# A hybrid decoder layer on one core: the order of work around the first pair of the feed-forward part

## The chip, the cores and the metric

One core of one Trainium2 chip runs the whole layer in one launch. The metric is the device time of a run in microseconds (us); several runs are timed and their median is given. One more execution is recorded by the profiler, and its time stands beside its span (from the first to the last instruction).

## What is computed

The input x has 512 tokens of 1024 channels. A layer norms it, projects it, runs four token mixers beside each other, merges them by gates, projects back and adds. Then comes the feed-forward part (FFN), which is what the change touches:

```python
def swiglu_ffn(h, w_gate, w_up, w_down):
    return (jax.nn.silu(h @ w_gate) * (h @ w_up)) @ w_down

x = x + merged @ w_out
h = rms_norm(x, ffn_norm[l])          # this is h2 below
x = x + swiglu_ffn(h, w_ffn_gate[l], w_ffn_up[l], w_ffn_down[l])
```

All is float32. D_FF is 2816.

## The kernel before

**Three products for one.** A float32 matrix is split into a high part in a reduced format that TensorE multiplies fast (made by ScalarE, ACT, with a copy) and a low part, the rest (made by VectorE, DVE, with a subtraction of the high part). One product is then three matmuls on TensorE (PE): high by high, high by low, low by high. So every operand of PE needs an ACT instruction, then a DVE instruction.

**h2.** The normed x is scaled by DVE (`scaled`, L1976), one tile of 128 tokens after another, t = 0 to 3. `turn_h2(t)` (L2669) is eight transposes on PE into two banks of PSUM, four for each; ACT makes the high part `f_hi` of each bank (`h2_high`, L1230), DVE the low part `f_lo` (`h2_low`, L1944). Tiles 0 and 1 are turned during the output projection, tiles 2 and 3 during the plain part below, at the place in the loop where the `if` at its end says so.

**The first pair, plain.** The FFN weights come in chunks of 256 columns, a gate chunk and an up chunk for each pair. The first pair is multiplied the plain way: `plain_part(up, half)` (L2716) does both column tiles (j = 0, 1) of one chunk for one half of the tokens, 8 steps k of 3 matmuls for each j, in the order gate/first half, up/first half, gate/second half, up/second half. Then ACT takes the gate tiles with Silu (`gated`, L1338, adds to `gate_taken`) and DVE multiplies them with the up tiles (`hidden`, L2111, adds to `up_taken`).

**The other pairs, Winograd.** `wino_chunk(c)` (L2747) does each further chunk as seven products of half-size blocks, 12 matmuls each. In order: 1 A11·B11, 2 S3·T3, 3 S2·T2, 4 A12·B21, 5 S1·T1, 6 A22·T4, 7 S4·B22. The T are sums of blocks of h2: `block_sums` (DVE, L2045 to L2055) makes the four, `block_high` (ACT, L1348) their high parts, `t_low` (DVE, L2059) their low parts, in the order T3, T2, T1, T4. The S are sums of blocks of the chunk's weights: `weight_sums` (DVE, L2070 to L2077; its step 0 is the first two, step 1 the other two). High parts of weights are made by ACT in four steps (`wino_split`, L1317 to L1326), low parts by DVE in four steps (`weight_lows`: step 0 L2084, step 1 L2089, steps 2 and 3 L2095). `split_ahead` does the steps of the next chunk while PE works on this one.

**Sums through PSUM.** Between the products, results are copied from bank to bank: after product 1 ACT seeds c11 (L1414); after product 2 ACT copies `seventh` (L1419); after product 3 DVE adds c21 (L2226, semaphore `c21_seeded`), for which PE waits ahead of product 5; after product 5 ACT copies c12 (L1428, `c12_seeded`), for which PE waits ahead of product 7; after product 6 DVE adds c22 (L2244).

**What sets the order.** Every engine has one list of instructions in the order of the code, and does them strictly in that order; semaphores hold an engine until another has come far enough. Nothing is scheduled by a planner. In ACT's list, in the first Winograd chunk (m = 0) alone, the high parts of the first hidden tiles stand ahead of the copy of c12:

```python
                split_ahead(c + 1, 1, 2, 3)
                if m == 0:
                    for j in range(CT):
                        hidden_high(0, j, j + 1)
                act.wait_ge(S["product_done"], 7 * m + 5)
                nact.activation(f0[:, T2ND], first[:, T1ST], ACT.Copy).then_inc(S["c12_seeded"], 1)
```

`hidden_high(0, j, j + 1)` (L1344) waits until `up_taken` has reached j + 1, that is for the (j + 1)th `hidden` of DVE.

Of the kernel before, what the change touches and what calls it, by code (L numbers as in the profile page):

```python
# [42 lines left out]
def hybrid_layer(nc, x, mix_norm, w_in, attn_q_norm, attn_k_norm, pool_w, pool_scale, gmlp_norm,  # L43
# [5 lines left out]
    KT = D // P  # L49
# [127 lines left out]
    WINO = [c for c in range(NC) if chunks[c][0] == "ffn"]  # L177
# [60 lines left out]
    with ExitStack() as ctx:  # L238
# [626 lines left out]
        def _(act):  # L865
# [462 lines left out]
            def split_ahead(c, *steps):  # L1328
                if c < NC and chunks[c][0] == "ffn":
                    for step in steps:  # L1330
                        wino_split(c, step)
                elif c < NC and 0 in steps:
                    split(c)
# [12 lines left out]
            def block_high(i):  # L1346
                act.wait_ge(S["t_made"], 4)
                nact.activation(t_hi[:, i], t_sum[:, i], ACT.Copy).then_inc(S["t_hi_ready"], 1)  # L1348
# [44 lines left out]
                split_ahead(part_at[1], 0, 1, 2, 3)  # L1393

            T1, T2, T3, T4 = range(4)
            act.wait_ge(filled, fill_at[PLAIN[0]] + 1)
            gated(0, 0, bank[2])
            block_high(T3)
            block_high(T2)
            act.wait_ge(filled, fill_at[PLAIN[0]] + CT)  # L1400
            gated(0, 1, bank[3])
            split_ahead(WINO[0], 0, 1)
            split_ahead(WINO[0], 2)
            block_high(T1)
            split_ahead(WINO[0], 3)
            block_high(T4)

            for c in WINO:
                m = wino_index[c]
                pair, up = pair_of(c)  # L1410
# [71 lines left out]
        def _(dve):  # L1482
# [574 lines left out]
            def t_low(i):  # L2057
                dve.wait_ge(S["t_hi_ready"], (T3, T2, T1, T4).index(i) + 1)
                vec.tensor_tensor(t_lo[:, i], t_sum[:, i], t_hi[:, i].bitcast(F32), ALU.subtract)\  # L2059
                    .then_inc(S["t_lo_ready"], 1)  # L2060
# [37 lines left out]
            def split_ahead(c, *steps):  # L2098
                if c < NC and chunks[c][0] == "ffn":
                    for step in steps:  # L2100
                        weight_lows(c, step)
                elif c < NC and 0 in steps:
                    split(c)
# [89 lines left out]

            block_sums()
            t_low(T3)
            dve.wait_ge(lo_ready, PLAIN[1] + 1)
            sums_ahead(WINO[0])
            split_ahead(WINO[0], 0)
            split_ahead(WINO[0], 2)
            t_low(T2)  # L2200
            split_ahead(WINO[0], 1)
            t_low(T1)
            split_ahead(WINO[0], 3)
            t_low(T4)

            for c in WINO:
# [19 lines left out]
                vec.tensor_tensor(f1[:, T1ST], first[:, T1ST], seventh[:, up, :], ALU.add).then_inc(S["c21_seeded"], 1)  # L2226
                if m == 0:
                    weight_sums(c + 1, (1,))
                    for j in range(CT):
                        dve.wait_ge(filled, fill_at[PLAIN[1]] + j + 1)  # L2230
                        hidden(0, j, bank[(fill_at[PLAIN[1]] + j) % 2])
                    split_ahead(c + 1, 0, 1)
                else:
                    split_ahead(c + 1, 0, 1, 2, 3)
                if c == F11 - 1:
# [7 lines left out]
                dve.wait_ge(S["c12_seeded"], m + 1)  # L2243
                vec.tensor_tensor(f1[:, T2ND], first[:, T1ST], seventh[:, up, :], ALU.add).then_inc(S["c22_ready"], 1)  # L2244
                if m == 0:
                    split_ahead(c + 1, 2, 3)
                if c == F11 - 2:

                    dve.wait_ge(S["up_taken"], CT * 2 * QT // CT)
# [72 lines left out]
        def _(pe):  # L2322
# [393 lines left out]
            def plain_part(up, half):  # L2716

                c = PLAIN[up]
                at = w_at(c)
                c_hi, c_lo = (p1_hi[:, :], p1_lo[:, :]) if up else (w_hi[:, at + HIGH_OFF:at + HIGH_OFF + CHUNK],  # L2720
                                                                    w_lo[:, at:at + CHUNK])
                cols = slice(half * SEQ // 2, (half + 1) * SEQ // 2)
                pe.wait_ge(hi_ready, c + 1)
                if up:
                    pe.wait_ge(S["out_lo"], len(OUT_SPLIT) + 1)
                else:
                    pe.wait_ge(lo_ready, c + 1)
                pe.wait_ge(S["h2_lo_ready"], TT * (half + 1) - 1)
                pe.wait_ge(S["x1_taken"], (8, OUT_ADDS)[up])
                for j in range(CT):  # L2730
                    b = bank[(fill_at[c] + j) % 2] if up else bank[2 + j]
                    for k in range(KT):
                        if j == 0 and k == KT // 2:
                            pe.wait_ge(S["h2_lo_ready"], TT * (half + 1))
                        w = slice(k * CW + j * P, k * CW + (j + 1) * P)
                        begin, end = k == 0 and half == 0, k == KT - 1
                        mm(b[:, cols], c_hi[:, w], f_hi[:, k, cols], start=begin, stop=False, skip_group_check=True)  # L2737
                        mm(b[:, cols], c_hi[:, w], f_lo[:, k, cols], start=False, stop=False, skip_group_check=True)  # L2738
                        last = mm(b[:, cols], c_lo[:, w], f_hi[:, k, cols], start=False, stop=end, skip_group_check=True)  # L2739
                        if up and (half, j) == (0, 0) and k in (0, KT // 2):  # L2740
                            turn_h2(2 + k // (KT // 2))
                    if half == 1:
                        last.then_inc(filled, 1)

# [119 lines left out]
```

## Time and profile before

| | |
|---|---|
| median of 3 runs | 759.77 us (759.62 to 760.0) |
| the profiled execution, its own time | 759.43 us |
| its span | 757.5 us |
| PE busy | 750.8 us (99%) |
| DVE busy | 591.0 us (78%) |
| ACT busy | 404.0 us (53%) |
| POOL busy | 105.4 us (14%) |
| granted clock of PE in the span | 1.00 |

A time of the profile is counted from the start of the span. The device time is the span and about 1.9 us around it. In the timeline a row is one instruction, or several alike (x2), with its start, its length, its line and its tiles; what stands in brackets is how long the engine had been idle and what released it. Matmuls overlap: a matmul of 256 columns is shown as 0.28 us long, while the next starts 0.11 us after it. The distance between the starts of two neighbours is called their spacing below. On DVE and ACT too, an instruction may start a little before the one ahead of it is shown as ended.

### The profile page before, as it was taken

The numbers are of one execution on the slowest core, as the hardware profiler recorded it, in microseconds if no ns is written. First come the engines' busy times: TensorE is split into PE (matmuls) and PEld (weight loads), VectorE is DVE, ScalarE is ACT, GpSimd is POOL, SyncE is SP. The second block draws the span as 40 slices with busy tenths as digits, with TensorE's granted clock in tenths as the row PEclk, the third lists the DMA queues.
The fourth block names the chain that finished last, engine by engine and source line by source line (L and its number), as shares of the span: only waits on it lengthen the run. The fifth ranks groups of instructions, "written<-read, shape, count | busy, mean of one in ns | idle before, by whom it ended". The sixth has DMA issues, their size and how long they took to land.

```text
span 757.5 us, 11636 instructions
## 1 busy us (share of the span) xinstructions
PE 750.8 (99%) x4590; PEld 665.7 (88%) x4590; DVE 591.0 (78%) x816; ACT 404.0 (53%) x603; POOL 105.4 (14%) x130
## 2 busy tenths in 40 slices
PE   8999999999999999999999999999999999999998
PEld 8988888988888888888888899999888999999886
DVE  5636989878788966425988889889989888888991
ACT  6645546456663654545349555565544556666430
POOL 7100040457203221221231000000000000000000
PEclk9999999999999999999999999999999999999999
DMA  8362213221133113317226624336063333338102
GB/s 280 100 188 73 92 58 112 69 100 55 56 112 111 56 60 109 112 55 274 88 85 174 186 112 137 109 105 236 0 250 112 112 113 112 112 113 315 73 29 84
DMA packets 67879, 89.56 MB, mean 118 GB/s; under 512 B 3109, under 2 KB 52593, under 8 KB 67697
## 3 DMA queue, kind: packets, MB, share of 16 engines
q1 hardware_dynamic: 66224, 85.60, 33.6%
q0 software_dynamic: 1456, 3.09, 2.0%
q8 instruction: 37, 0.61, 0.3%
q10 hardware_dynamic: 144, 0.13, 0.1%
q14 instruction: 18, 0.14, 0.1%
HBM read 81.99 MB, written 4.19 MB: 114 GB/s over the span
## 4 chain that ended last, share of the span: by engine, by line
PE 96%; DVE 1%; ACT 1%; issue 1%; POOL 1%; DVEq 0%; POOLq 0%
PE bank L2327 14%; PE bank L2329 14%; PE bank L2328 14%; PE bank L2765 8%; PE bank L2766 8%; PE bank L2767 8%; PE bank L2827 5%; PE bank L2831 5%; PE bank L2829 5%; PE bank L2708 2%; PE bank L2707 2%; PE bank L2706 2%; PE bank L2737 1%; PE bank L2738 1%; PE bank L2739 1%
## 5 line engine op out<-in xcount | busy, mean ns | idle before, releaser
L2327 PE MATMUL bank<-h_hi,w_hi 128*128 128x512 f32 (+1 forms) x352 | 134.7, 383 | 0.2 <-DVE w_lo L1569 0.2
L2329 PE MATMUL bank<-h_hi,w_lo 128*128 128x512 f32 (+1 forms) x352 | 133.7, 380 | 0.0
L2328 PE MATMUL bank<-h_lo,w_hi 128*128 128x512 f32 (+1 forms) x352 | 133.6, 379 | 0.0
L1497 DVE TENSOR_TENSOR w_lo<-raw,w_hi 128x2048 fp32r<-128x2048 f32 x30 | 71.0, 2371 | 39.7 <-ACT w_hi L881 31.8
L2765 PE MATMUL bank<-t_hi,w_hi 128*128 128x256 f32 x320 | 88.4, 276 | 1.1 <-DVE bank L2226 1.1
L2766 PE MATMUL bank<-t_lo,w_hi 128*128 128x256 f32 x320 | 88.3, 276 | 0.0
L2767 PE MATMUL bank<-t_hi,w_lo 128*128 128x256 f32 x320 | 88.3, 276 | 0.0
L2327 PEld LDWEIGHTS bank<-h_hi,w_hi 128*128 128x128 f32 x352 | 66.2, 188 | 12.6 <-ACT w_hi L944 0.4
L2329 PEld LDWEIGHTS bank<-h_hi,w_lo 128*128 128x128 f32 x352 | 66.2, 188 | 12.6
L2328 PEld LDWEIGHTS bank<-h_lo,w_hi 128*128 128x128 f32 x352 | 66.2, 188 | 12.1
L2765 PE MATMUL bank<-f_hi,w_hi 128*128 128x256 f32 x240 | 66.4, 277 | 0.3 <-ACT bank L1428 0.3
L2766 PE MATMUL bank<-f_lo,w_hi 128*128 128x256 f32 x240 | 66.3, 276 | 0.0
L2767 PE MATMUL bank<-f_hi,w_lo 128*128 128x256 f32 x240 | 66.3, 276 | 0.0
L2765 PEld LDWEIGHTS bank<-t_hi,w_hi 128*128 128x128 f32 x320 | 60.1, 188 | 1.3 <-issue 1.3
L2767 PEld LDWEIGHTS bank<-t_hi,w_lo 128*128 128x128 f32 x320 | 60.1, 188 | 0.0
L2766 PEld LDWEIGHTS bank<-t_lo,w_hi 128*128 128x128 f32 x320 | 60.1, 188 | 0.0
L849 POOL TENSOR_TENSOR merged<-merged,two 128x512 f32<-128x512 f32 x24 | 37.3, 1558 | 161.9 <-DVE two L1875 161.9
L881 ACT ACTIVATE w_hi<-raw 128x2048 fp32r<-128x2048 f32 x28 | 53.8, 1925 | 0.2 <-DMA raw<-in_w_in_dram 0.2
L1071 ACT ACTIVATE two<-bank 128x512 f32<-128x512 f32 x24 | 14.4, 599 | 65.0 <-PE bank L2329 58.3
L2095 DVE TENSOR_TENSOR w_lo<-w_sum,w_hi 128x1024 fp32r<-128x1024 f32 x40 | 47.1, 1217 | 0.0
L2827 PE MATMUL bank<-w_hi,a_hi 128*128 128x512 f32 x120 | 46.8, 390 | 0.0
L2829 PE MATMUL bank<-w_lo,a_hi 128*128 128x512 f32 x120 | 46.7, 389 | 0.0
(357 smaller groups left out, 1862.4 us busy)
## 6 DMA issues: line engine op xcount, KB each, us to landing
raw<-in_w_in_dram SPq DMA_DIRECT2D x26, 1024.0 KB, 4.9
raw<-in_w_ffn_up_dram SPq DMA_DIRECT2D x11, 1024.0 KB, 5.1
raw<-in_w_ffn_gate_dram SPq DMA_DIRECT2D x10, 1024.0 KB, 5.1
raw<-in_w_ffn_down_dram SPq DMA_DIRECT2D x7, 1024.0 KB, 5.0
raw<-in_w_branch_dram SPq DMA_DIRECT2D x4, 1024.0 KB, 4.7
b<-in_w_ffn_down_dram SPq DMA_DIRECT2D x4, 1024.0 KB, 6.8
x_sb<-in_x_dram SPq DMA_DIRECT2D x6, 512.0 KB, 4.6
o<-in_w_out_dram SPq DMA_DIRECT2D x3, 1024.0 KB, 9.9
```

The costliest lines, as they stand in the source:

```text
L881: nact.activation(w_hi[:, at:at + n], raw[:, c % 2, 0:n], ACT.Copy).then_inc(hi_ready, 1)
L1497: vec.tensor_tensor(w_lo[:, at], raw[:, c % 2, 0:n], w_hi[:, high].bitcast(F32), ALU.subtract)\
L2095: vec.tensor_tensor(quad(w_lo, c, s, 2), quad(w_sum, c, s, 2), quad(w_hi, c, s, 2).bitcast(F32), ALU.subtract).then_inc(S["quad_lo_ready"], 1)
L2327: mm(dst, l_hi, r_hi, start=start, stop=False)
L2328: mm(dst, l_hi, r_lo, start=False, stop=False)
L2329: return mm(dst, l_lo, r_hi, start=False, stop=stop)
L2765: mm(dst, l_hi, r_hi, start=begin and k == 0, stop=False, skip_group_check=True)
L2766: mm(dst, l_hi, r_lo, start=False, stop=False, skip_group_check=True)
L2767: ins = mm(dst, l_lo, r_hi, start=False, stop=k == KT // 2 - 1, skip_group_check=True)
L2827: mm(bank[banks[t]][:, :], l_hi[:, k, rows], w_hi[:, w], start=anew and k == 0, stop=False, skip_group_check=True)
L2829: mm(bank[banks[t]][:, :], l_hi[:, k, rows], w_lo[:, w], start=False, stop=False, skip_group_check=True)
L2831: ins = mm(bank[banks[t]][:, :], l_lo[:, k, rows], w_hi[:, w], start=False, stop=k == tiles - 1, skip_group_check=True)
```

## The change

It moves instructions on three engines; none is added or taken out.

- PE: `turn_h2(2)` stood after step k = 0 of the first tile of the up chunk, and now stands after step k = 4 of the last tile (j = 1) of the gate chunk, which is 12 matmuls sooner. `turn_h2(3)` stood after step k = 4 of the up chunk's first tile and now stands after step k = 1: 9 matmuls sooner.
- ACT: the high parts of T3, T2 and T1 stand ahead of both gate tiles; before, T3 and T2 stood between the two, and T1 between the steps of the first Winograd chunk's weights.
- DVE: the low parts of T3, T2 and T1 stand in a row ahead of the sums of the first Winograd chunk's weights. In that chunk, steps 0 and 2 of the next chunk's low parts stand ahead of the two `hidden`; before, they stood behind them.

```diff
--- before.py
+++ after.py
@@ -1393,16 +1393,14 @@
                 split_ahead(part_at[1], 0, 1, 2, 3)
 
             T1, T2, T3, T4 = range(4)
+            block_high(T3)
+            block_high(T2)
+            block_high(T1)
             act.wait_ge(filled, fill_at[PLAIN[0]] + 1)
             gated(0, 0, bank[2])
-            block_high(T3)
-            block_high(T2)
             act.wait_ge(filled, fill_at[PLAIN[0]] + CT)
             gated(0, 1, bank[3])
-            split_ahead(WINO[0], 0, 1)
-            split_ahead(WINO[0], 2)
-            block_high(T1)
-            split_ahead(WINO[0], 3)
+            split_ahead(WINO[0], 0, 1, 2, 3)
             block_high(T4)
 
             for c in WINO:
@@ -2193,14 +2191,11 @@
 
             block_sums()
             t_low(T3)
+            t_low(T2)
+            t_low(T1)
             dve.wait_ge(lo_ready, PLAIN[1] + 1)
             sums_ahead(WINO[0])
-            split_ahead(WINO[0], 0)
-            split_ahead(WINO[0], 2)
-            t_low(T2)
-            split_ahead(WINO[0], 1)
-            t_low(T1)
-            split_ahead(WINO[0], 3)
+            split_ahead(WINO[0], 0, 2, 1, 3)
             t_low(T4)
 
             for c in WINO:
@@ -2226,10 +2221,11 @@
                 vec.tensor_tensor(f1[:, T1ST], first[:, T1ST], seventh[:, up, :], ALU.add).then_inc(S["c21_seeded"], 1)
                 if m == 0:
                     weight_sums(c + 1, (1,))
+                    split_ahead(c + 1, 0, 2)
                     for j in range(CT):
                         dve.wait_ge(filled, fill_at[PLAIN[1]] + j + 1)
                         hidden(0, j, bank[(fill_at[PLAIN[1]] + j) % 2])
-                    split_ahead(c + 1, 0, 1)
+                    split_ahead(c + 1, 1)
                 else:
                     split_ahead(c + 1, 0, 1, 2, 3)
                 if c == F11 - 1:
@@ -2243,7 +2239,7 @@
                 dve.wait_ge(S["c12_seeded"], m + 1)
                 vec.tensor_tensor(f1[:, T2ND], first[:, T1ST], seventh[:, up, :], ALU.add).then_inc(S["c22_ready"], 1)
                 if m == 0:
-                    split_ahead(c + 1, 2, 3)
+                    split_ahead(c + 1, 3)
                 if c == F11 - 2:
 
                     dve.wait_ge(S["up_taken"], CT * 2 * QT // CT)
@@ -2737,8 +2733,10 @@
                         mm(b[:, cols], c_hi[:, w], f_hi[:, k, cols], start=begin, stop=False, skip_group_check=True)
                         mm(b[:, cols], c_hi[:, w], f_lo[:, k, cols], start=False, stop=False, skip_group_check=True)
                         last = mm(b[:, cols], c_lo[:, w], f_hi[:, k, cols], start=False, stop=end, skip_group_check=True)
-                        if up and (half, j) == (0, 0) and k in (0, KT // 2):
-                            turn_h2(2 + k // (KT // 2))
+                        if (up, half, j, k) == (0, 0, 1, KT // 2):
+                            turn_h2(2)
+                        elif (up, half, j, k) == (1, 0, 0, 1):
+                            turn_h2(3)
                     if half == 1:
                         last.then_inc(filled, 1)
 
```

How the lists change, first DVE ahead of the first Winograd chunk. `t_lo` are the low parts of T, `w_sum` the sums of the weights' blocks, `w_lo` low parts of weights. Before:

```order
L2059 TENSOR_TENSOR t_lo<-t_sum,t_hi 128x1024 [waits t_hi_ready]
L2070 TENSOR_TENSOR w_sum<-raw 128x512 [waits filled,raw1,lo_ready]
L2071 TENSOR_TENSOR w_sum<-raw 128x512
L2075 TENSOR_TENSOR w_sum<-w_sum,raw 128x512 [waits sum_made]
L2077 TENSOR_TENSOR w_sum<-raw,w_sum 128x512 [waits sum_made]
L2084 TENSOR_TENSOR w_lo<-raw,w_hi 128x1024 [waits quad_hi_ready]
L2095 TENSOR_TENSOR w_lo<-w_sum,w_hi 128x1024 [waits quad_hi_ready,sum_made]
L2059 TENSOR_TENSOR t_lo<-t_sum,t_hi 128x1024 [waits t_hi_ready]
L2089 TENSOR_TENSOR w_lo<-raw,w_hi 128x512 [waits hi_ready]
L2059 TENSOR_TENSOR t_lo<-t_sum,t_hi 128x1024 [waits t_hi_ready]
L2095 TENSOR_TENSOR w_lo<-w_sum,w_hi 128x1024 [waits quad_hi_ready,sum_made]
L2059 TENSOR_TENSOR t_lo<-t_sum,t_hi 128x1024 [waits t_hi_ready]
```

Now (the file is two to five lines shorter, so its numbers are lower):

```order
L2057 TENSOR_TENSOR t_lo<-t_sum,t_hi 128x1024 [waits t_hi_ready] x3
L2068 TENSOR_TENSOR w_sum<-raw 128x512 [waits filled,raw1,lo_ready]
L2069 TENSOR_TENSOR w_sum<-raw 128x512
L2073 TENSOR_TENSOR w_sum<-w_sum,raw 128x512 [waits sum_made]
L2075 TENSOR_TENSOR w_sum<-raw,w_sum 128x512 [waits sum_made]
L2082 TENSOR_TENSOR w_lo<-raw,w_hi 128x1024 [waits quad_hi_ready]
L2093 TENSOR_TENSOR w_lo<-w_sum,w_hi 128x1024 [waits quad_hi_ready,sum_made]
L2087 TENSOR_TENSOR w_lo<-raw,w_hi 128x512 [waits hi_ready]
L2093 TENSOR_TENSOR w_lo<-w_sum,w_hi 128x1024 [waits quad_hi_ready,sum_made]
L2057 TENSOR_TENSOR t_lo<-t_sum,t_hi 128x1024 [waits t_hi_ready]
```

The second and third `t_lo` went ahead of the four sums; the fourth stayed behind.

DVE in the first Winograd chunk, `a_sum` being the two `hidden` of the plain pair. Before:

```order
L2070 TENSOR_TENSOR w_sum<-raw 128x512 [waits filled,raw0]
L2071 TENSOR_TENSOR w_sum<-raw 128x512
L2226 TENSOR_TENSOR bank<-bank,seventh 128x256 [waits gate_taken,seventh_copied,product_done]
L2075 TENSOR_TENSOR w_sum<-w_sum,raw 128x512 [waits sum_made]
L2077 TENSOR_TENSOR w_sum<-raw,w_sum 128x512 [waits sum_made]
L2111 TENSOR_TENSOR a_sum<-bank,act_158 128x512 [waits gate_taken,filled] x2
L2084 TENSOR_TENSOR w_lo<-raw,w_hi 128x1024 [waits quad_hi_ready]
L2089 TENSOR_TENSOR w_lo<-raw,w_hi 128x512 [waits hi_ready]
L2244 TENSOR_TENSOR bank<-bank,seventh 128x256 [waits c12_seeded,product_done]
L2095 TENSOR_TENSOR w_lo<-w_sum,w_hi 128x1024 [waits quad_hi_ready,sum_made] x2
```

Now:

```order
L2068 TENSOR_TENSOR w_sum<-raw 128x512 [waits filled,raw0]
L2069 TENSOR_TENSOR w_sum<-raw 128x512
L2221 TENSOR_TENSOR bank<-bank,seventh 128x256 [waits gate_taken,seventh_copied,product_done]
L2073 TENSOR_TENSOR w_sum<-w_sum,raw 128x512 [waits sum_made]
L2075 TENSOR_TENSOR w_sum<-raw,w_sum 128x512 [waits sum_made]
L2082 TENSOR_TENSOR w_lo<-raw,w_hi 128x1024 [waits quad_hi_ready]
L2093 TENSOR_TENSOR w_lo<-w_sum,w_hi 128x1024 [waits quad_hi_ready,sum_made]
L2109 TENSOR_TENSOR a_sum<-bank,act_158 128x512 [waits gate_taken,filled] x2
L2087 TENSOR_TENSOR w_lo<-raw,w_hi 128x512 [waits hi_ready]
L2240 TENSOR_TENSOR bank<-bank,seventh 128x256 [waits c12_seeded,product_done]
L2093 TENSOR_TENSOR w_lo<-w_sum,w_hi 128x1024 [waits quad_hi_ready,sum_made]
```

Two `w_lo` of 1024 columns (steps 0 and 2) stand ahead of the two `a_sum`; one of 512 (step 1) and one of 1024 (step 3) stand behind them.

ACT, from the last high parts of h2 to the first copy between banks. `act_158` is a gate tile. Before:

```order
L1230 ACTIVATE f_hi<-bank 128x4x128 [waits h2_turned] x4
L1338 ACTIVATE act_158<-bank 128x512 [waits filled,out_tile]
L1348 ACTIVATE t_hi<-t_sum 128x1024 [waits t_made] x2
L1338 ACTIVATE act_158<-bank 128x512 [waits filled]
L1317 ACTIVATE w_hi<-raw 128x1024 [waits filled,raw1]
L1320 ACTIVATE w_hi<-raw 128x512
L1323 ACTIVATE w_hi<-w_sum 128x1024 [waits sum_made]
L1348 ACTIVATE t_hi<-t_sum 128x1024 [waits t_made]
L1326 ACTIVATE w_hi<-w_sum 128x1024 [waits sum_made]
L1348 ACTIVATE t_hi<-t_sum 128x1024 [waits t_made]
L1414 ACTIVATE bank<-bank 128x256 [waits gate_taken,product_done]
```

Now:

```order
L1230 ACTIVATE f_hi<-bank 128x4x128 [waits h2_turned] x4
L1348 ACTIVATE t_hi<-t_sum 128x1024 [waits t_made,out_tile]
L1348 ACTIVATE t_hi<-t_sum 128x1024 [waits t_made] x2
L1338 ACTIVATE act_158<-bank 128x512 [waits filled] x2
L1317 ACTIVATE w_hi<-raw 128x1024 [waits filled,raw1]
L1320 ACTIVATE w_hi<-raw 128x512
L1323 ACTIVATE w_hi<-w_sum 128x1024 [waits sum_made]
L1326 ACTIVATE w_hi<-w_sum 128x1024 [waits sum_made]
L1348 ACTIVATE t_hi<-t_sum 128x1024 [waits t_made]
L1412 ACTIVATE bank<-bank 128x256 [waits gate_taken,product_done]
```

Three `t_hi` stand ahead of the first gate tile. Behind this piece ACT's list is the same in both.

## Rows read from the trace of the kernel before

**Rows 1.** The page of the profile: its head, and the busy time of each engine

```profile
span 757.5 us, 11636 instructions
...
PE 750.8 (99%) x4590; PEld 665.7 (88%) x4590; DVE 591.0 (78%) x816; ACT 404.0 (53%) x603; POOL 105.4 (14%) x130
```

**Rows 2.** Waits of PE over the span: total us, times, longest

```profile
PE bank L2765 <- DVE bank L2226: 1.1, 1, 1.1
...
PE bank L2765 <- ACT bank L1428: 0.3, 1, 0.3
```

**Rows 3.** Timeline of PE, first Winograd chunk: start us, us, operation, [idle before <-releaser]

```profile
452.67 0.28 PE L2765 MATMUL bank<-f_hi,w_hi 128*128 128x256 f32 x1
...
458.00 0.28 PE L2767 MATMUL bank<-f_hi,w_lo 128*128 128x256 f32 x1
459.37 0.36 PE L2765 MATMUL bank<-t_hi,w_hi 128*128 128x256 f32 x1 [1.10 <-DVE bank L2226]
...
462.07 0.28 PE L2767 MATMUL bank<-t_hi,w_lo 128*128 128x256 f32 x1
462.68 0.39 PE L2765 MATMUL bank<-f_hi,w_hi 128*128 128x256 f32 x1 [0.34 <-ACT bank L1428]
```

**Rows 4.** The chain of waits, two pieces: start us, us, engine, tile, line

```profile
460.80 0.89 ACT w_hi L1326
...
461.96 0.40 ACT a_hi L1344
```

**Rows 5.** Timeline of PE: the two groups of transposes of h2

```profile
434.84 1.03 PE L2678 MATMUL bank<-ident,h 128*128 128x128 f32 x8
...
437.13 1.03 PE L2678 MATMUL bank<-ident,h 128*128 128x128 f32 x8
```

**Rows 6.** Timeline of DVE, from the scaling of h2 to the gatings

```profile
433.64 1.28 DVE L1976 SCALAR_TENSOR_TENSOR h<-x_sb,rstd,ffn_gain 128x1024 f32<-128x1024 f32 x1
...
438.40 1.29 DVE L1944 TENSOR_TENSOR f_lo<-bank,f_hi 128x512 fp32r<-128x512 f32 x2 [1.00 <-ACT f_hi L1230]
...
443.38 1.22 DVE L2055 TENSOR_TENSOR t_sum<-h2T,t_sum 128x1024 f32<-128x1024 f32 x1
446.35 1.23 DVE L2059 TENSOR_TENSOR t_lo<-t_sum,t_hi 128x1024 fp32r<-128x1024 f32 x1 [1.76 <-ACT t_hi L1348]
447.53 0.69 DVE L2070 TENSOR_TENSOR w_sum<-raw 128x512 f32<-128x512 f32 x1
...
450.07 1.22 DVE L2084 TENSOR_TENSOR w_lo<-raw,w_hi 128x1024 fp32r<-128x1024 f32 x1
451.21 1.22 DVE L2095 TENSOR_TENSOR w_lo<-w_sum,w_hi 128x1024 fp32r<-128x1024 f32 x1
...
458.69 0.42 DVE L2226 TENSOR_TENSOR bank<-bank,seventh 128x256 f32<-128x256 f32 x1
...
460.35 1.28 DVE L2111 TENSOR_TENSOR a_sum<-bank,act 128x512 f32<-128x512 f32 x2
```

**Rows 7.** Timeline of ACT in the same stretch

```profile
445.27 2.00 ACT L1348 ACTIVATE t_hi<-t_sum 128x1024 fp32r<-128x1024 f32 x2
...
461.66 0.70 ACT L1344 ACTIVATE a_hi<-a_sum 128x256 fp32r<-128x256 f32 x2
462.27 0.36 ACT L1428 ACTIVATE bank<-bank 128x256 f32<-128x256 f32 x1
```

**Rows 8.** Timeline of DVE two chunks later

```profile
473.28 1.33 DVE L2111 TENSOR_TENSOR a_sum<-bank,act 128x512 f32<-128x512 f32 x2
...
478.00 0.43 DVE L2226 TENSOR_TENSOR bank<-bank,seventh 128x256 f32<-128x256 f32 x1 [0.86 <-PE bank L2767]
```

**Rows 9.** Timeline of ACT two chunks later

```profile
474.01 0.42 ACT L1344 ACTIVATE a_hi<-a_sum 128x256 fp32r<-128x256 f32 x1 [2.44 <-DVE a_sum L2111]
```

**Rows 10.** Stretch of the first Winograd chunk: busy of each engine, PEclk, DMA

```profile
452.67:464.10 11.43, 9.99 (x86) 9.63 (x85) 11.39 (x16) 6.19 (x11) 0.00 (x0) 1.00 0.29 93
```

## The prediction

> **What bounds the kernel now.** I read the busy times first: PE is busy for 750.8 of 757.5 us [rows 1]. There is no other bound to look for: the change can win only what PE stands still, or lose by new waits of PE. The table of PE's waits [rows 2] shows how little that is: in the whole FFN part there are two waits, one for DVE's add of c21 (L2226, 1.1 us) and one for ACT's copy of c12 (L1428, 0.3 us). The timeline of PE puts both into the first Winograd chunk and gives their full price [rows 3]. From 452.67 to 458.00 lie 47 spacings, so one is 5.33 / 47 = 0.113 us and a product of 12 matmuls takes 1.36 us. Product 5 could have started at 458.00 + 0.11 = 458.11 and starts at 459.37: 1.26 us lost. Product 7 could have started at 462.07 + 0.11 = 462.18 and starts at 462.68: 0.50 us lost. Between the two, product 5 and 6 took 0.09 us more than 2 x 1.36, since the first matmul after a stop is slow. Without any wait product 7 would start at 458.11 + 2.72 = 460.83; it starts at 462.68. **So 1.85 us, 0.24% of the time, is all that can be won.** I call 0.2%, 1.5 us, what a measurement of this kernel can tell from no change.
>
> Who makes PE wait? DVE has no idle time from 446.35 on [rows 6]; its add of c21 starts at 458.69, although PE's third product was done long before. The chain of waits goes on through ACT: high parts of weights, high parts of the hidden tiles, then the copy of c12 [rows 4]. On ACT the two high parts `a_hi` stand directly ahead of that copy, at 461.66 and 462.27 [rows 7]. That order I follow below, since the change does not alter it.
>
> **The transposes, sooner.** Turn 2 moves up by 12 spacings, from 434.84 [rows 5] to 433.48; turn 3 by 9, at 0.113 to 0.12 us each by 1.02 to 1.08, I take 1.05: from 437.13 to 436.08. PE does the same instructions, so this costs it nothing unless it now waits. Turn 3 needs the last scaling, which starts at 433.64 and ends at 434.92 [rows 6]; 1.16 us are left. Turn 2 needs the scaling before that one, which is ended when this one runs, by about 433.7 at the latest; the scalings are each some 1.2 us apart from the next, so I take it as done by 432.5. Cost: nothing; if the cover were gone, the wait would be about 0.2 us. What turn 3 starts, the low parts of h2 (438.40) and the sums of its blocks (the last at 443.38), follows it by 1.05: the last sum starts at 442.33 and ends at 443.55.
>
> **ACT, three high parts ahead of the gate tiles.** Before, the first T high part started at 445.27 [rows 7], behind a gate tile, although the sums were complete at 443.38 + 1.22 = 444.60 [rows 6]. Now it starts at 443.6. The gate tiles come later by less than the three high parts (0.95 apart, from 2.00 for two), at 446.5 and then as before; nobody needs them before product 1 is done, at 452.67 + 1.36 = 454.03 [rows 3]. Cost: nothing.
>
> **DVE, three low parts ahead of the sums.** The first low part came 1.08 us after its high part's start (445.27 to 446.35) [rows 6, 7], so now at 444.68. Three of them at 1.14 each (450.07 to 451.21 is one instruction of that size) and the weights' sums start at 448.10, where they started at 447.53: 0.57 later. The low part of A11, which product 1 waits for, starts 2.54 us behind that (447.53 to 450.07), at 450.64, and ends at 451.86; PE wants it at 452.67 [rows 3]. 0.8 us of cover are left. From the first sum to the add of c21 lay 458.69 - 447.53 = 11.16 us without idle time; two low parts (2.28) no longer lie there, so it is 8.88, and DVE comes to the add at 456.98. PE's third product ends at 452.67 + 35 x 0.113 + 0.28 = 456.91, so DVE and PE meet. The add comes 1.71 us sooner than before. Its release reached PE 0.68 us later (458.69 to 459.37): 457.66, ahead of 458.11. **The wait ahead of product 5 goes: 1.26 us, and with the slow restart 1.35 us.** That such a lead is enough is seen two chunks later, where the add waits for PE [rows 8] and PE never for it [rows 2].
>
> **DVE, the next low parts ahead of the gatings.** This is the part that costs. Before, the first `hidden` (`a_sum`, L2111) started 1.66 us behind the add of c21 (458.69 to 460.35) [rows 6]. Now two low parts of 1024 columns stand between, 1.14 each: 1.66 + 2.28 = 3.94, so it starts at 456.98 + 3.94 = 460.92, 0.57 later than before, in spite of all that was won. The second follows at 0.60, at 461.52. Behind it stands ACT: `a_hi` starts 0.73 us after its `a_sum` when it waits for it (473.28 to 474.01) [rows 8, 9], so the second at 462.25. Two `a_hi` and the copy of c12 are 0.61 / 2 = 0.31 apart (461.66 to 462.27) [rows 7]: the copy starts at 462.56, where product 5 would allow it from 459.7 on. PE started product 7 0.41 us after the copy's start (462.27 to 462.68) [rows 3, 7]: **462.97, against 462.68 before.** A wait of 2.14 us stands where 1.85 us stood in two.
>
> **The sum.** The stall ahead of product 5: -1.26. The slow restart behind it: -0.09. The stall ahead of product 7: from 0.50 to 462.97 - 460.83 = 2.14, +1.64. Together +0.29 us. What comes behind product 7 follows PE: DVE's steps 1 and 3 of the next chunk end sooner or by 0.3 later than before, and PE wants the last of them only with product 5 of that chunk, some five microseconds on. The bounds of what I had to infer: the hand-over from `a_sum` to `a_hi` is 0.73 where ACT waits and cannot be under the 0.68 that the instruction lasts; the shift of turn 3 is 1.02 to 1.08; the spacing of DVE's instructions may be a few hundredths off over 14 of them. All together -0.2 to +0.4 around the sum. The profiled execution would go from 759.43 to 759.72 us, with a span of 757.8; its own time was 0.34 below the median, and against the median of 759.77 I forecast **760.1 us, no change that can be measured**.
>
> **The clock.** In this stretch the granted clock is 1.00, the level of 2.4 GHz, through stops of 1.10 and 0.34 us [rows 3, 10]. The new stop is longer than either. The Trainium skill says (TensorE: Matmul & The Clock Gate, section "HAM oscillation — how this bites in real kernels") that idle stretches between bursts of matmuls can send the array back to its lower clock. The trace agrees only so far that stops up to 1.10 us did not; by that rule the sum would be as in rival C, by the rows it is +0.29.
>
> **Rivals.**
> A, faster: the gatings' delay does not reach PE, and both waits go. That would be so if the copy of c12 did not stand behind the two `a_hi`, or DVE passed the four instructions much faster. Then 1.85 us are won: 757.9 us. For it speaks that DVE's low parts have to be made anyway and come off the way to c21; against it speaks ACT's strict order in the list and its chain [rows 4, 7]. Between A and my forecast each tenth that DVE gains ahead of the `hidden` is a tenth for PE. Chance 0.05.
> B, the earlier transposes do nothing for the sums (something else, such as ACT's change of table or the scaling, holds the high parts of h2). Then the T sums end at 444.60 as before, the first low part starts at 445.73, and everything down to product 7 is 1.05 us later: 464.0, that is 1.3 over before, 761.1 us. Against it: both turns keep 1 us of cover to the scalings [rows 5, 6]. Chance 0.04, and it stays just within 0.2%.
> C, slower: the stop of 2.14 us ahead of product 7 lets the clock fall to 1.2 GHz. It decides from the first product done at that level: spacing doubles, so each product costs 1.36 us more. Lower end: one product, 0.29 + 1.36 = +1.65, 761.4 us. Upper end: a chunk of seven, +9.8, 769.6. I take the lower end as its price, since the trace has no stretch at the lower level [rows 10] and the nearest stops cost nothing. Chance 0.03.
>
> **How the numbers follow.** My forecast has 0.88: 760.1 us, by its own bounds 759.9 to 760.5, and as the runs before spread over 0.4 us, 759.6 to 760.8. The range reaches to B: 759.5 to 761.1; A and C stay out. Faster by over 0.2%: A, 0.05. Slower by over 0.2%: C and a little of B with a further slip, 0.04. Within: 0.91.
>
> **What the profile would show.** Right: PE's only wait in the first Winograd chunk is for L1426 (the copy of c12 in the new numbers), of about 2 us, and product 5 starts without one; the sums of weights start at about 448.1, the add of c21 at 457.0, the `a_sum` at 460.9, and ACT shows idle time ahead of `a_hi`, released by `a_sum`. Wrong: a copy of c12 that starts before 462; a wait ahead of product 1 or 5; a granted clock under 1.00 behind the stop.

## The result and the profile after

| | before | changed |
|---|---|---|
| median | 759.81 us (20 runs, 759.44 to 760.67) | 761.56 us (20 runs, 759.75 to 762.22) |
| ratio | | 1.0018 (95% interval 1.0012 to 1.0024) |
| profiled execution, its own time | 759.43 us | 759.75 us |
| its span | 757.5 us | 757.8 us |
| runs with a mean granted clock under 0.999 | 2 of 89, beside the experiments below | 13 of 20 |

The change made the kernel slower by 1.75 us in the medians. The runs of the changed kernel do not lie around one value. Seven have a mean granted clock of 1.000 and a median of 759.92 us; thirteen have 0.998 and a median of 761.84. The profiled execution is one of the seven, and its rows are those that were forecast, to a few hundredths of a microsecond. The page of its profile:

```profile
span 757.8 us, 11636 instructions
...
PE 750.2 (99%) x4590; PEld 665.1 (88%) x4590; DVE 591.2 (78%) x816; ACT 404.4 (53%) x603; POOL 105.9 (14%) x130
```

The span is 0.3 us longer. In the table of PE's waits one row stands in the FFN part, where [rows 2] had two:

```profile
PE bank L2763 <- ACT bank L1426: 2.0, 1, 2.0
```

The timeline of PE in the first Winograd chunk (start us, us, operation), which answers to [rows 3]: product 1 begins, product 5 begins, product 6 begins its last matmul, product 7 begins.

```profile
452.59 0.28 PE L2763 MATMUL bank<-f_hi,w_hi 128*128 128x256 f32 x1
...
458.03 0.28 PE L2763 MATMUL bank<-t_hi,w_hi 128*128 128x256 f32 x1
...
460.64 0.28 PE L2765 MATMUL bank<-t_hi,w_lo 128*128 128x256 f32 x1
462.95 0.38 PE L2763 MATMUL bank<-f_hi,w_hi 128*128 128x256 f32 x1 [2.04 <-ACT bank L1426]
```

Product 5 starts on time, 48 spacings behind product 1. Product 7 could start at 460.64 + 0.11 = 460.75 and starts at 462.95: 2.20 us lost in one piece, where before 1.85 were lost in two.

The timeline of DVE, which answers to [rows 6]:

```profile
437.29 1.29 DVE L1942 TENSOR_TENSOR f_lo<-bank,f_hi 128x512 fp32r<-128x512 f32 x2 [1.26 <-ACT f_hi L1230]
...
442.27 1.22 DVE L2053 TENSOR_TENSOR t_sum<-h2T,t_sum 128x1024 f32<-128x1024 f32 x1
444.68 3.50 DVE L2057 TENSOR_TENSOR t_lo<-t_sum,t_hi 128x1024 fp32r<-128x1024 f32 x3 [1.19 <-ACT t_hi L1348]
448.09 0.68 DVE L2068 TENSOR_TENSOR w_sum<-raw 128x512 f32<-128x512 f32 x1
...
456.98 0.42 DVE L2221 TENSOR_TENSOR bank<-bank,seventh 128x256 f32<-128x256 f32 x1
...
458.63 1.22 DVE L2082 TENSOR_TENSOR w_lo<-raw,w_hi 128x1024 fp32r<-128x1024 f32 x1
459.77 1.22 DVE L2093 TENSOR_TENSOR w_lo<-w_sum,w_hi 128x1024 fp32r<-128x1024 f32 x1
460.90 1.28 DVE L2109 TENSOR_TENSOR a_sum<-bank,act 128x512 f32<-128x512 f32 x2
```

The low parts of h2 and the last sum of its blocks (442.27) are 1.11 sooner, of which 0.08 are this execution's earlier start of the whole stretch; the three low parts of T from 444.68, the sums of the weights at 448.09, the add of c21 at 456.98, then the two low parts of 1024 columns ahead of the gatings, and these (`a_sum`) at 460.90.

The timeline of ACT, which answers to [rows 7]:

```profile
443.58 2.96 ACT L1348 ACTIVATE t_hi<-t_sum 128x1024 fp32r<-128x1024 f32 x3 [5.84 <-DVE t_sum L2053]
...
461.62 0.42 ACT L1344 ACTIVATE a_hi<-a_sum 128x256 fp32r<-128x256 f32 x1 [1.58 <-DVE a_sum L2109]
462.21 0.42 ACT L1344 ACTIVATE a_hi<-a_sum 128x256 fp32r<-128x256 f32 x1 [0.18 <-DVE a_sum L2109]
462.54 0.36 ACT L1426 ACTIVATE bank<-bank 128x256 f32<-128x256 f32 x1
```

Both `a_hi` now wait for their `a_sum` (1.58 and 0.18 us idle), and the copy of c12 behind them starts at 462.54, 0.41 ahead of product 7. It was free to start when product 5 ended, at about 459.7.

### The profile page after: what moved, and what is told of

It reads as the page before. It is cut to its first block, busy times and chain, and to the rows that moved or that the text cites. A ratio compares the mean times of both kernels' runs of the same rounds, so it can differ in the third digit from the quotient of the medians.

```text
span 757.8 us, 11636 instructions
## 1 busy us (share of the span) xinstructions
PE 750.2 (99%) x4590; PEld 665.1 (88%) x4590; DVE 591.2 (78%) x816; ACT 404.4 (53%) x603; POOL 105.9 (14%) x130
## 4 chain that ended last, share of the span: by engine, by line
PE 95%; DVE 2%; issue 1%; ACT 1%; POOL 1%; DMA 1%; DVEq 0%; SPq 0%; POOLq 0%
PE bank L2323 14%; PE bank L2325 14%; PE bank L2324 14%; PE bank L2763 8%; PE bank L2764 8%; PE bank L2765 8%; PE bank L2825 5%; PE bank L2827 5%; PE bank L2829 5%; PE bank L2704 2%; PE bank L2703 2%; PE bank L2702 2%; PE bank L2734 1%; PE bank L2735 1%; PE bank L2733 1%
## 5 line engine op out<-in xcount | busy, mean ns | idle before, releaser
L2763 PEld LDWEIGHTS bank<-f_hi,w_hi 128*128 128x128 f32 x240 | 45.1, 188 | 2.3 <-ACT bank L1426 2.2
```

Of the source, the lines that this page charges most:

```text
L2763: mm(dst, l_hi, r_hi, start=begin and k == 0, stop=False, skip_group_check=True)
```

## The experiments

Theory 1: PE's stop of 2.2 us costs its length, and in a part of the executions it also lets the granted clock fall to 1.2 GHz for a while. Rival: the longer executions come from something else in the change. Each kernel was run beside the kernel before on the same chip. In every one the order of some instructions is altered, or matmuls are added whose result nobody reads; all of them compute the whole layer.

**The changed kernel as it is.** No edit, so that a profile of a longer execution could be caught.

> The changed kernel as it is. Theory 1: PE's one stop of about 2.3 us between product 6 and product 7 lets the granted clock fall in some executions; these take about 1.8 us longer. So the times fall into two groups, near 759.9 us with a mean clock of 1.000 and near 761.8 us with 0.998, and a profile from the second shows a stretch of lower clock right behind 463. Rival: the longer executions have another cause (a transfer, a late release elsewhere), and a profile of one shows lost time somewhere else.

Measured: 12 runs, ratio 1.0019 (1.0005 to 1.0033). Six at 1.000 with a median of 760.03 us, six at 0.998 with 762.36. The profile fell on one of the six, with a span of 760.2. Its stretches of 1 us behind the stop (length, busy us of PE, PEld, DVE, ACT, POOL with counts, PEclk, DMA share, GB/s):

```profile
464.00:465.00 1.00, 1.00 (x11) 1.00 (x11) 1.00 (x2) 0.60 (x1) 0.00 (x0) 1.00 0.15 29
465.00:466.00 1.00, 1.00 (x8) 1.00 (x7) 0.69 (x2) 0.45 (x1) 0.00 (x0) 0.51 0.81 236
466.00:467.00 1.00, 1.00 (x6) 1.00 (x6) 1.00 (x3) 0.15 (x1) 0.00 (x0) 0.50 1.09 389
467.00:468.00 1.00, 1.00 (x7) 1.00 (x6) 0.96 (x2) 0.00 (x0) 0.00 (x0) 0.50 1.02 364
468.00:469.00 1.00, 1.00 (x9) 1.00 (x8) 0.24 (x1) 0.89 (x2) 0.00 (x0) 0.78 0.10 32
469.00:470.00 1.00, 1.00 (x11) 1.00 (x10) 0.00 (x0) 0.69 (x2) 0.00 (x0) 1.00 0.00 0
```

And its timeline of PE:

```profile
461.37 0.28 PE L2765 MATMUL bank<-t_hi,w_lo 128*128 128x256 f32 x1
463.71 0.39 PE L2763 MATMUL bank<-f_hi,w_hi 128*128 128x256 f32 x1 [2.06 <-ACT bank L1426]
...
465.31 0.41 PE L2763 MATMUL bank<-f_hi,w_hi 128*128 128x256 f32 x1
465.52 0.41 PE L2764 MATMUL bank<-f_lo,w_hi 128*128 128x256 f32 x1
...
468.49 0.28 PE L2763 MATMUL bank<-t_hi,w_hi 128*128 128x256 f32 x1
468.60 0.28 PE L2764 MATMUL bank<-t_lo,w_hi 128*128 128x256 f32 x1
```

The stop lies from 461.5 to 463.71. PE goes on at full pace, eleven matmuls in the microsecond from 464. At about 465.0 the granted clock falls to 0.50, the spacing goes from 0.113 to 465.52 - 465.31 = 0.21, six to eight matmuls in a microsecond, and at 468.4 it is over. Between 465.10 and 468.49 lie 16 spacings, 3.39 us instead of 1.81: 1.6 us lost. The other 0.8 us by which this span is longer were there before the stop, which lies 0.76 us later than in the first profile (463.71 against 462.95); from run to run the part ahead of the FFN varies by that much. Three more profiles below (the changed kernel again, and the kernels moved by 12 and by 24 matmuls) fell on executions with the lower clock. All four show the same: full pace behind the stop for 0.3 to 1.3 us, then 15 or 16 slow spacings, 1.5 to 1.6 us lost.

The table also shows a burst of transfers in just this stretch. Such a burst is neither enough for the fall nor needed for it. The profile of the changed kernel at full clock has the burst too, without a fall:

```profile
465.50:466.00 0.50, 0.50 (x7) 0.50 (x6) 0.50 (x2) 0.00 (x0) 0.00 (x0) 1.00 1.09 389
```

And in the kernel moved by 24 matmuls the clock is down before the burst begins:

```profile
466.00:466.50 0.50, 0.50 (x5) 0.50 (x4) 0.50 (x2) 0.36 (x1) 0.00 (x0) 0.50 0.00 0
```

The forecast of the stretch holds, the rival falls; what remains to be shown is that the idle time is the cause.

**The stop filled with work.** 16 matmuls between product 6 and the wait.

```diff
                 product(f1[:, T1ST], A22, T4, False)
+                if m == 0:
+                    for _ in range(16):
+                        mm(bank[4][:, T2ND], w_hi[:, w_at(c) + hi_pad(c):w_at(c) + hi_pad(c) + P], t_hi[:, T4, 0, :],
+                           start=True, stop=True, skip_group_check=True)
                 pe.wait_ge(S["c12_seeded"], m + 1)
```

> The changed kernel with 16 more matmuls of 256 columns (1.8 us of work) on PE between product 6 and the wait for c12, into a half of a bank that nobody reads. The wait ends when it did. Theory 1 (the idle of PE is what lets the clock fall): one group of times near 759.9 us, clock 1.000 in every run, though 16 matmuls are added. Rival (the longer group comes from something else in the change): two groups as in the changed kernel, 759.9 and 761.8 us.

Measured: 12 runs, median 760.02 us (759.52 to 760.57), all at 0.999 or 1.000, ratio 1.0000 (0.9992 to 1.0008). Its timeline of PE:

```profile
460.36 0.28 PE L2765 MATMUL bank<-t_hi,w_lo 128*128 128x256 f32 x1
460.47 1.98 PE L2798 MATMUL bank<-t_hi,w_hi 128*128 128x256 f32 x16
462.69 0.39 PE L2763 MATMUL bank<-f_hi,w_hi 128*128 128x256 f32 x1 [0.25 <-ACT bank L1426]
```

The wait for the copy is where it was, but PE is idle for 0.25 us only. With more work on the busiest engine the median is 0.6 us lower than that of the changed kernel on the same chip (760.60) and 1.5 us lower than in its first series, and the group at 762 us is gone: 0 of 12 runs, where the changed kernel had 6 of 12 on this chip. All that the change moved is still in this kernel, so PE's idleness is what the fall needs. It is not all that decides it: further below, kernels with a stop as long have a fall in one run of eight and one of eleven.

**The gatings ahead of the next lows again**, the rest as changed.

```diff
-                    split_ahead(c + 1, 0, 2)
                     for j in range(CT):
...
-                    split_ahead(c + 1, 1)
+                    split_ahead(c + 1, 0, 1)
...
-                    split_ahead(c + 1, 3)
+                    split_ahead(c + 1, 2, 3)
```

> The earlier turns and the three lows ahead of the sums stay; the gatings stand ahead of the next lows again. Both gatings then start at 457.0 + 1.66 = 458.6, the copy of c12 behind ACT's high parts at about 460.55, product 7 at about 460.96. Theory 1: PE loses 0.2 us there and nothing ahead of product 5, the clock stays at 1.000 in every run, one group of times near 757.9 us, 1.9 under before. Rival: the two groups stay, 1.8 us apart, since the stop is not their cause.

Measured: 12 runs, median 758.05 us, ratio 0.9983 (0.9969 to 0.9996); one of the twelve stood apart at 763.53 with 0.998, so "in every run" was missed by one. Three of the 32 runs of the kernel before that were taken beside it stood apart too (762.9 to 765.1, two of them at 0.998). The one is 5.5 us above its kernel, far more than a fall behind the stop costs, so it does not speak of the stop. Its timeline of PE around product 7:

```profile
460.90 0.28 PE L2764 MATMUL bank<-t_hi,w_lo 128*128 128x256 f32 x1
461.24 0.39 PE L2762 MATMUL bank<-f_hi,w_hi 128*128 128x256 f32 x1
```

461.24 - 460.90 - 0.11 = 0.23 us are lost, as expected, and 1.8 us are won over the kernel before. So the first two parts of the change do what they should; the third, the low parts ahead of the gatings, turned the gain into a loss.

**ACT's copy of c12 ahead of its two high parts**, the rest as changed.

```diff
+                act.wait_ge(S["product_done"], 7 * m + 5)
+                nact.activation(f0[:, T2ND], first[:, T1ST], ACT.Copy).then_inc(S["c12_seeded"], 1)
                 if m == 0:
                     for j in range(CT):
                         hidden_high(0, j, j + 1)
-                act.wait_ge(S["product_done"], 7 * m + 5)
-                nact.activation(f0[:, T2ND], first[:, T1ST], ACT.Copy).then_inc(S["c12_seeded"], 1)
```

> The changed kernel with ACT's copy of c12 ahead of its two high parts of the hidden tiles; DVE's list untouched. Theory 1: the copy starts at about 459.6, PE stops at neither product, span about 755.6, one group of times near 757.7 us, clock 1.000. Rival (DVE itself is what holds PE, not ACT's place behind the gatings): product 7 stays at 462.95 and the time at 760 to 762 us.

Measured: 9 runs, median 757.72 us (757.46 to 758.38), ratio 0.9961 (0.9942 to 0.9981), all at 1.000; no wait of PE in the FFN part is left. Its timeline of ACT (this execution runs 0.35 us later in the span than the profiled one of the changed kernel):

```profile
460.29 0.37 ACT L1423 ACTIVATE bank<-bank 128x256 f32<-128x256 f32 x1
461.97 0.42 ACT L1344 ACTIVATE a_hi<-a_sum 128x256 fp32r<-128x256 f32 x1 [1.32 <-DVE a_sum L2109]
```

The copy starts at 460.29 (459.6 expected; it stands behind ACT's last high part of weights), and the `a_hi` wait for DVE behind it, where nobody on PE waits for them. With all of the change kept and this one block moved, the kernel is 2.1 us faster than before. **It beats both kernels**, the changed one by 2.9 us in the medians on the same chip (757.72 against 760.60).

**The same move in the kernel before.**

> The kernel before with ACT's copy of c12 ahead of its two high parts of the hidden tiles. The copy then starts behind ACT's last high part of weights, at about 461.7, in time for product 7; the wait ahead of product 5 stays. 0.50 us less than before: near 759.3 us, one group. Rival (the copy's wait is on product 5 itself, not on its place): no change.

Measured: 11 runs, median 759.24 us beside 759.46 for the kernel before, ratio 0.9997 (0.9988 to 1.0005). The wait for the copy is gone from the table of PE's waits, the 1.1 us ahead of product 5 stay, and the profiled span is 757.1 us, 0.4 under the one of before. The sign is the one expected. Of the size, 0.50, the medians show 0.2 and the two profiled spans 0.4, and the interval takes in no change.

**One low part ahead of the gatings**, and then **three**: the length of the stop varied. The diff is that of the first; the second has the steps 0, 2, 1 there. A step that is taken away from there stands where it stood in the kernel before.

```diff
-                    split_ahead(c + 1, 0, 2)
+                    split_ahead(c + 1, 0)
```

> The changed kernel with only step 0 of the next lows ahead of the gatings (1.14 us instead of 2.28). Product 7 starts 1.14 us sooner; PE loses about 1.1 us there, so near 758.8 us at full clock. Theory 1 (the clock falls only behind a stop that is long enough): at about 1.1 us, as long as the stops of the kernel before, no run shows a lower clock: one group. Rival (any stop at that place can let the clock fall): some runs at 0.998, about 1.8 us above the others.

> The changed kernel with steps 0, 2 and 1 ahead of the gatings: 0.60 us more on DVE, so product 7 starts 0.6 later and PE loses about 2.8 us there; near 760.5 us at full clock. Theory 1: the longer stop lets the clock fall in a larger share of the runs than the 19 of 32 of the changed kernel, near 762.3 us; the median goes up by more than 0.6. Rival: the share does not grow with the stop.

Measured with one: 11 runs, median 759.12 us beside 759.86, ratio 0.9997 (0.9985 to 1.0009), since one run at 763.85 (0.997) lies among them; ten runs are at 1.000 with a median of 759.09. The one is 4.8 us above them, like those that stood apart above and unlike the falls behind the long stops, so it neither confirms nor refutes that a stop of 1.1 us is harmless. Its PE:

```profile
461.06 0.28 PE L2765 MATMUL bank<-t_hi,w_lo 128*128 128x256 f32 x1
462.25 0.39 PE L2763 MATMUL bank<-f_hi,w_hi 128*128 128x256 f32 x1 [0.92 <-ACT bank L1426]
```

1.08 us lost, as expected. With three: 11 runs, median 761.90, ratio 1.0022 (1.0014 to 1.0031). Five at 1.000 with 760.52, six at 0.998 with 762.54. Its PE:

```profile
460.71 0.28 PE L2764 MATMUL bank<-t_hi,w_lo 128*128 128x256 f32 x1
463.65 0.39 PE L2762 MATMUL bank<-f_hi,w_hi 128*128 128x256 f32 x1 [2.66 <-ACT bank L1426]
```

2.83 us lost. At full clock each kernel stands within 0.3 us of its expected time. The mean clock was lower in that one of eleven behind a stop of 1.1 us, in 28 of all 43 runs of the changed kernel behind 2.2 us, in six of eleven behind 2.8 us. The share did not grow from 2.2 to 2.8; that part of the expectation was missed.

**The lows ahead of the gatings alone**, in the kernel before.

> The kernel before with this part alone: steps 0 and 2 of the next lows ahead of the gatings. The stop ahead of product 5 stays at 1.26; both gatings start 2.28 later, at 462.63 and 463.23, the copy of c12 at 464.27, product 7 at 464.68 instead of 462.68: PE loses 2.5 us there, the time at full clock is 2.0 over before, near 761.8 us. Theory 1: with a stop of 2.5 us the clock falls in most runs, and these are near 763.5 us. Rival (the part is hidden by DVE's own lateness): 759.8 us as before.

Measured: 11 runs, median 761.83 us, ratio 1.0029 (1.0021 to 1.0038). Eight at 1.000 with a median of 761.65, three at 0.998 with 763.35. Its PE:

```profile
459.30 0.36 PE L2766 MATMUL bank<-t_hi,w_hi 128*128 128x256 f32 x1 [1.10 <-DVE bank L2226]
...
464.61 0.39 PE L2766 MATMUL bank<-f_hi,w_hi 128*128 128x256 f32 x1 [2.31 <-ACT bank L1428]
```

Product 7 starts at 464.61 (464.68 expected), so this part alone costs 1.9 us, and nothing of it is hidden. The two levels of time are right, but the clock fell in three of eleven, not in most as expected.

**Both turns of h2 at their old places**, the rest as changed. The diff is the part on PE, undone.

> The changed kernel with both turns of h2 at their old places, all else as changed. The sums of h2's blocks are 1.05 later and DVE's whole list down to product 7 with them: add of c21 at about 458.0, a stop of 0.6 ahead of product 5, product 7 at about 464.0; near 761.0 us at full clock, and 762.8 where it falls, which it does in most runs by theory 1 (stop of 2.6 us ahead of product 7). Rival (the sooner turns bring nothing, the high parts are held by something else): times as of the changed kernel.

Measured: 11 runs, median 761.16 us (761.0 expected at full clock), ratio 1.0018 (1.0009 to 1.0026). One of the eleven at 0.998, where most were expected. Its waits of PE:

```profile
PE bank L2761 <- ACT bank L1426: 2.3, 1, 2.3
...
PE bank L2761 <- DVE w_lo L2082: 0.3, 1, 0.3
```

At full clock it is 1.2 us slower than the changed kernel (761.13 against 759.92), so the sooner turns are worth that, through DVE's list. The place of the wait was partly missed: I had expected 0.6 us ahead of product 5. Instead PE waits ahead of product 1 for the low part of A11 (0.3 us idle), and is late from there on. The first matmul of product 1 starts 0.55 us behind the one ahead of it, so 0.44 are lost; that of product 5, which waits for the add of c21, 0.24 behind, so 0.13 are lost:

```profile
453.35 0.36 PE L2761 MATMUL bank<-f_hi,w_hi 128*128 128x256 f32 x1 [0.27 <-DVE w_lo L2082]
...
459.01 0.36 PE L2761 MATMUL bank<-t_hi,w_hi 128*128 128x256 f32 x1
```

The 0.8 us of cover that the prediction gave that low part is less than the 1.05 that the turns had moved.

**The whole moved in time.** Since the share of fallen clocks followed neither theory, 12 and then 24 matmuls were put ahead of the plain part. The stop stays as long and comes later.

```diff
                 pe.wait_ge(S["x1_taken"], (8, OUT_ADDS)[up])
+                if (up, half) == (0, 0):
+                    for _ in range(12):
+                        mm(bank[2][:, cols], c_hi[:, 0:P], f_hi[:, 0, cols], start=True, stop=True, skip_group_check=True)
                 for j in range(CT):
```

> The changed kernel once more, beside the two shifted ones on the same chip. So far 19 of its 32 runs had the lower clock. Expected: about 6 in 10 again, near 759.9 and 761.8 us.

> The changed kernel with 12 more matmuls (1.36 us) ahead of the plain part, so that everything from there on, the stop of 2.3 us too, comes 1.36 us later in the span and is as long as it was. Near 761.3 us at full clock, 763.1 where the clock falls. Theory 1a (the length of the stop decides the share): 6 in 10 again. Theory 1b (it also matters where the stop lies in time): the share goes well up or down.

> The same with 24 more matmuls, 2.72 us: near 762.7 us at full clock, 764.5 where it falls. Theory 1a: 6 in 10 fall. Theory 1b: another share than in the changed kernel or in the one shifted by 1.36 us.

Measured on one chip: the changed kernel again, 11 runs, nine of them at 0.998 with a median of 762.04 us, ratio 1.0026 (1.0017 to 1.0035). Moved by 12 matmuls: 8 runs, one at 0.998, median 761.46, ratio 1.0026 (1.0015 to 1.0036). Moved by 24: 5 runs, three at 0.998, median 764.09, ratio 1.0055 (1.0042 to 1.0069). In all three the profile shows PE idle for 2.05 or 2.06 us at the stop, and the lower clock behind it. Of the changed kernel, whose PE goes on at 463.05:

```profile
463.00:463.50 0.50, 0.45 (x3) 0.45 (x4) 0.40 (x2) 0.00 (x0) 0.00 (x0) 1.00 0.00 0
463.50:464.00 0.50, 0.50 (x5) 0.50 (x4) 0.50 (x2) 0.43 (x1) 0.00 (x0) 0.60 0.04 14
```

So the kernel with 1.36 us more work has a lower median than the one without it (761.46 against 762.01). One in eight against 28 in 43 speaks for theory 1b, that it matters where the stop lies in time. The table below says the same when it is read by place, a grouping made after the fact: where product 7 starts between 462.9 and 463.7, the clock fell in 34 of 54 runs (the changed kernel and the one with three lows); with as long a stop and product 7 between 463.9 and 464.7 (moved by 12, late turns, lows alone) it fell in 5 of 30; later still in 3 of 5. But the changed kernel's own profiles spread over 0.8 us, and these kernels differ in more than the place. I call theory 1b likely and not shown.

| kernel | lost ahead of product 7, us | product 7 starts, us | clock fell | median, clock 1.000 | median, clock lower |
|---|---|---|---|---|---|
| changed (three series) | 2.20 | 462.95 | 28 of 43 | 759.92 | 761.96 |
| stop filled | under 0.3 idle | 462.69 | 0 of 12 | 760.02 | |
| gatings first | 0.23 | 461.24 | 1 of 12 | 758.03 | 763.53 |
| copy first | none | | 0 of 9 | 757.72 | |
| one low | 1.08 | 462.25 | 1 of 11 | 759.09 | 763.85 |
| three lows | 2.83 | 463.65 | 6 of 11 | 760.52 | 762.54 |
| lows alone | 2.49 | 464.61 | 3 of 11 | 761.65 | 763.35 |
| late turns | 2.50 | 464.32 | 1 of 11 | 761.13 | 763.15 |
| moved by 12 | 2.23 | 463.95 | 1 of 8 | 761.45 | 762.44 |
| moved by 24 | 2.22 | 465.62 | 3 of 5 | 763.30 | 764.12 |

The starts of product 7 are those of one profiled execution each; the same kernel moves by some tenths from one execution to the next (462.95, 463.05 and 463.71 for the changed one). Taken together, the clock was lower in 42 of 89 runs of the kernels that lose 2.2 us or more ahead of product 7. It was lower in 4 of 144 runs of all the others, the kernel before among them with 2 of 89; those four stood 4.6 us or more above the median of their kernels, more than a fall costs. What disturbed them no run shows.

## Why the prediction was wrong

- **What bounds the kernel: right.** PE's waits were the whole account. With both of them gone the kernel stands 2.1 us under before, where 1.85 was said to be all there is (1.7 in the profiled spans, 755.8 against 757.5); the interval of that ratio (1.4 to 4.4 us) holds it.
- **The transposes: right.** Turn 3 brought the sums of h2 1.11 us sooner (1.05 forecast), without a wait on PE. The experiment with late turns prices it at 1.2 us in the medians.
- **Three high and three low parts ahead: right.** First low part at 444.68 (444.68), sums of weights at 448.09 (448.10), add of c21 at 456.98 (456.98), no wait ahead of product 5.
- **The lows ahead of the gatings: right.** `a_sum` at 460.90 (460.92), second `a_hi` at 462.21 (462.25), the copy at 462.54 (462.56), product 7 at 462.95 (462.97). The part alone costs 1.9 us.
- **The sum at full clock: right.** +0.29 forecast, +0.3 in the spans of the profiles, and +0.1 in the medians (759.92 of the runs at 1.000 against 759.81). 760.1 us was forecast for these runs, 759.92 measured.
- **The clock: here it failed.** The step was the sentence on rival C, "the nearest stops cost nothing", and the chance of 0.03 drawn from it. The stops between matmuls that the trace of before showed in the FFN were 1.10 and 0.34 us idle; the new one has 2.04. (There is one of 1.59 us at the start of the span, but no matmul stands ahead of it.) I had written that it is longer than either, and then used them as if they spoke for it. No row bore on 2 us, so nothing allowed a chance as small as 0.03; what the runs showed is a fall in 28 of 43. The place, the mechanism and the sign of rival C are those of the measured kernel. Its price was "one product at the lower level" (1.36, with the sum +1.65), 761.4 us; measured are 761.56 as the median and 761.84 in the runs where it happened. What one such fall costs is 761.84 - 759.92 = 1.9 us in the first series, of which 1.6 are the spacing at 1.2 GHz by the trace. That the price came out near is luck: no row told how long the clock stays low, and the 16 slow spacings lay close to the 12 that I had taken as the lower end.
- **The range: wrong through the same step.** 759.5 to 761.1 left rival C out. The Trainium skill says (TensorE: Matmul & The Clock Gate, section "HAM oscillation — how this bites in real kernels") that idle stretches between bursts can send the array to its lower clock; the prediction set this against the trace and dropped it. The trace of the changed kernel agrees in kind, with a clock of 0.50 from 465 to 468.4 behind an idle stretch of 2.06 us. It does not agree in size: the example of that section has waits of about 3 to 5 us, so the page alone did not foretell a fall behind 2.1 us, as the prediction had it.
- **Rival A** (757.9) is what the kernel with the copy ahead does: 757.72. Its reason was named rightly, the copy's place behind the two `a_hi`.

What stays open: why the same stop lets the clock fall in nine of eleven runs at one place and in one of eight 1.36 us later; and why the two groups of a kernel lie 0.8 to 2.7 us apart, where each of the four profiles with a fall loses 1.5 to 1.6 us by the slow spacing.

## What to carry to other kernels

Where two short stops of PE are merged into one, do not count their sum alone. Here a stop of about 2 us brought the clock down in 28 of 43 runs, and in the first series that cost another 1.9 us where it happened, so the median jumped where the profiled execution showed nothing. Look at the mean clocks of all runs, not at one profile. And before an instruction is moved on one engine, read what stands behind its reader on the next: here a copy of 0.36 us that PE needed stood behind two instructions that nobody needed soon. In the changed kernel, moving that copy turned a loss into a gain of 2.1 us over the kernel before; in the kernel before, the same move brought at most 0.5.

## What the runs showed of the hardware

The granted clock did not fall during the stop but after PE had gone back to work: 1.3, 0.5, 1.2 and 0.3 us after it in the four profiles that show a fall. It stayed at 0.50 for 3.4 us in each, although PE was busy all that time. Sixteen matmuls without a use, put into the stop, kept the mean clock at 0.999 or above in 12 of 12 runs. And the same kernel on the same chip has runs with a fall and runs without: two at 1.000 and nine at 0.998.
